# A root multiplied as the exponential's scale: attention with the q norm kept out of q, in a four-layer kernel

## The reference

```python
def rms_norm(x, g):
    return x * lax.rsqrt(jnp.mean(x * x, axis=-1, keepdims=True) + 1e-6) * g

def even_layer(x, ...):
    h = rms_norm(x, norm_g); proj = h @ w_in            # aq ak av ag bq bk bv bg
    aq = apply_rope(rms_norm(aq, a_qn)); ak = apply_rope(rms_norm(ak, a_kn))
    ya = sliding_window_sink_attention(aq, ak, av, sinks) * silu(ag)   # 8 q heads, 2 k heads
    bq = rms_norm(bq, b_qn); bk = rms_norm(bk, b_kn)                   # 8 heads, no rope
    yb = chunked_relbias_attention(bq, bk, bv, b_rel) * silu(bg)
    return x + concat(ya, yb) @ w_out

def odd_layer(x, ...):
    h = rms_norm(x, norm_g); q, k, v, gate = split(h @ w_in)
    q, k = rms_norm(q, qn), rms_norm(k, kn)             # 8 heads x 2 x 64
    s1, s2 = rope(q1) @ rope(k1).T / 8, rope(q2) @ rope(k2).T / 8      # masked by chunks of 64
    o = (softmax(s1) - lam * softmax(s2)) @ v
    y = rms_norm(o, subln_g) * (1 - lambda_init) * silu(gate)
    return x + y @ w_out
```

## Time and profile before

| | |
|---|---|
| median of 3 runs | 1959.96 us (1957.76 to 1960.65) |
| profiled execution, first to last instruction | 1956.6 us |
| so outside that span, against the median | 3.4 us |
| PE busy | 1926.3 us, 98% |
| DVE, ACT, POOL busy | 53%, 51%, 49% |
| first layer, second layer (about) | to 285 us, to 580 us |

### The profile page before, as it was taken

One profiled execution on the slowest core, in us unless ns is written; L12 is line 12 of the kernel. 1 busy time (PEld: TensorE's weight loads), 2 busy tenths in 40 slices (PEclk: granted clock), 3 DMA queues, 4 the chain that ended last, 5 costly groups with the idle time before them and its releaser, 6 DMA issues.

```text
span 1956.6 us, 26922 instructions
## 1 busy us (share of the span) xinstructions
PE 1926.3 (98%) x10034; PEld 1595.6 (82%) x10034; DVE 1028.6 (53%) x1879; ACT 1001.6 (51%) x1770; POOL 952.7 (49%) x1238
## 2 busy tenths in 40 slices
PE   9999999999999999999999999999999999999998
PEld 7877787887788888888788888888889888888887
DVE  4366545666644776576656644402646584444214
ACT  5477546666744555666346444412656364444323
POOL 5542256554554444443554555555543455555553
PEclk9999999999999999999999999999999999999999
DMA  5321122322222222222222232333222223222332
GB/s 201 102 66 53 45 87 87 94 79 81 77 82 95 66 76 76 83 69 76 87 91 91 93 105 97 94 89 100 79 65 63 76 77 107 97 97 97 91 96 73
DMA packets 55379, 169.32 MB, mean 87 GB/s; under 512 B 7120, under 2 KB 14032, under 8 KB 55120
## 3 DMA queue, kind: packets, MB, share of 16 engines
q1 hardware_dynamic: 54960, 167.50, 27.1%
q10 hardware_dynamic: 288, 0.10, 0.0%
HBM read 158.66 MB, written 2.10 MB: 82 GB/s over the span
## 4 chain that ended last, share of the span: by engine, by line
PE 91%; DVE 5%; ACT 2%; POOL 1%; issue 1%; DMA 0%; SPq 0%; ACTq 0%; DVEq 0%
PE ps L1976 23%; PE ps L1979 23%; PE ps L1977 23%; PE ps L2032 3%; PE ps L1988 3%; PE ps L2047 3%; PE ps L1991 2%; PE ps L1989 2%; PE ps L2040 2%; PE ps L2016 1%; PE ps L2026 1%; PE ps L2130 1%; POOL wl L2724 1%; PE ps L2001 1%; PE ps L2004 1%
## 5 line engine op out<-in xcount | busy, mean ns | idle before, releaser
L2724 POOL TENSOR_TENSOR wl<-st,wh 128x256 fp32r<-128x256 f32 (+1 forms) x1180 | 883.6, 780 | 945.8 <-ACT wh L2154 945.1
L1976 PE MATMUL ps<-xh,wh 128*128 128x512 f32 x1432 | 583.5, 407 | 2.5 <-DVE tmp L2412 1.9
L1979 PE MATMUL ps<-xh,wl 128*128 128x512 f32 x1432 | 559.3, 391 | 0.0
L1977 PE MATMUL ps<-xl,wh 128*128 128x512 f32 x1432 | 558.5, 390 | 0.0
L2154 ACT ACTIVATE wh<-st 128x1024 fp32r<-128x1024 f32 (+2 forms) x311 | 314.1, 1011 | 439.3 <-PE ps L1979 390.8
L1976 PEld LDWEIGHTS ps<-xh,wh 128*128 128x128 f32 x1432 | 269.2, 188 | 63.1 <-issue 9.2
L1979 PEld LDWEIGHTS ps<-xh,wl 128*128 128x128 f32 x1432 | 268.8, 188 | 57.6
L1977 PEld LDWEIGHTS ps<-xl,wh 128*128 128x128 f32 x1432 | 269.5, 188 | 54.6 <-issue 5.3
L2683 DVE SCALAR_TENSOR_TENSOR tmp<-ps,vec,tmp 128x510 f32<-128x510 f32 (+1 forms) x176 | 131.2, 749 | 206.5 <-ACT tmp L2333 203.5
L2641 DVE SCALAR_TENSOR_TENSOR res<-res,ps 128x512 f32<-128x512 f32 (+1 forms) x37 | 22.7, 614 | 216.5 <-PE ps L1979 208.2
L1976 PE MATMUL ps<-fa_h,wh 128*128 128x512 f32 x308 | 119.8, 389 | 0.0
(11 more groups left out here) (296 smaller groups left out, 3367.5 us busy)
## 6 DMA issues: line engine op xcount, KB each, us to landing
st<-in_f_up SPq DMA_DIRECT2D x88, 512.0 KB, 3.2
st<-in_o_fm SPq DMA_DIRECT2D x32, 512.0 KB, 3.5
st<-in_s_xbc SPq DMA_DIRECT2D x32, 512.0 KB, 3.5
st<-in_f_dn SPq DMA_DIRECT2D x32, 512.0 KB, 3.5
st<-in_e_fm SPq DMA_DIRECT2D x21, 512.0 KB, 3.5
st<-in_s_z SPq DMA_DIRECT2D x16, 512.0 KB, 3.5
st<-in_s_out SPq DMA_DIRECT2D x16, 512.0 KB, 3.6
tmp<-tmp SPq DMA_DIRECT2D x100, 64.0 KB, 2.0
```

Source lines behind the costliest of these rows:

```text
L1976: e.matmul(u.bank.ap, hi, x.h[:, kk, :], start=first, stop=False)
L1977: e.matmul(u.bank.ap, hi, x.l[:, kk, :], start=False, stop=False)
L1979: e.matmul(u.bank.ap, lo, x.h[:, kk, :], start=False, stop=last).then_inc(S["mm"], 1)
L2724: e.tensor_tensor(P.mem["wl"][w.m % NWR][:, part], P.mem["stage"][w.m % NSTAGE][:, part], P.mem["wh"][w.m % NWR][:, part].bitcast(F32), AL ...
```

## The change

For 12 q units (4 of the first layer's A heads and the 8 of the second layer) the root is no longer multiplied into q. ACT copies the unit with the gain as scale (`q_gain`), and the bank is free when that and the squares are done. The squares are summed per token with the tokens on the partitions: `q_sum`, four matmuls whose stationary side is a 128x128 block of the squares and whose moving side is 2 columns of the matrix of ones. The root of 128x8 numbers (`ln`, `rs`, with 64e-6 for 1e-6, which gives the root with the factor 1/8) stays in a new ring of three small tiles, and is a number per query there. The exponential takes it as its scale, per partition; its bias is minus the greatest score times the root (`mx`, `mx_r`). So the scores of these heads keep their sign, and the mask is minus the large number. The 4 q units of the B heads keep the old way, with the factor -1/8 in the gain.

In the second layer the first three units are k, v, q, where they were q, v, k. Five small kinds of instruction are merged into two (`neg`, `lam`), with the same work.

```diff
+    "pe": (..., "blk", "q_sum", "score", ...
+           "sums": 168, "rec": 177, "q_sum": 480, "mx_r": 160, ...
-        self.turns = ring(["turn0", "turn1"])
+        self.turns, self.roots = ring(["turn0", "turn1"]), ring(mem["rq"])
+        if kind in ("ln", "rs") and n == 8:
+            return 220
+    def q_prep_g(self, u, gain, loaded, pool, done):
+        g = yield from self.taken(self.tmp)
+        g.ready = [(yield ("q_gain", g, u, gain, loaded))]
+        s = yield from self.taken(self.tmp)
+        a = yield ("qsq", s, u)
+        u.bank.release(a, g.ready[0])
+        self.start(4, self.q_root_g(s, a, done))
+        g = yield from self.rope_g(g)
+        dst = yield from self.taken(pool)
+        g.release(*(yield from self.split_q_g(g.ap, g.ready, dst)))
+        done("q", dst)
+    def q_root_g(self, s, squared, done):
+        bank = yield from self.taken(self.aux)
+        t = yield ("q_sum", bank, s, [squared, self.shapes])
+        s.release(t)
+        r = yield from self.taken(self.roots)
+        a = yield ("ln", r.ap, bank.ap[:, 0:8], 1.0, self.c(C_E64, 1), t, r.freed, 8)
+        bank.release(a)
+        r.ready = [(yield ("rs", r.ap, r.ap, a, 8))]
+        done("r", r)
...
 (second layer)
-            prep(0, "qvk"[j], u)
+            prep(0, "kvq"[j], u)
-        yield from P.proj_border_g(x, [w[8], w[24], w[16]], first)
+        yield from P.proj_border_g(x, [w[16], w[24], w[8]], first)
...
-                t = yield ("mn", mn.ap[:, 2 * i:2 * i + 2], g.s, t, mn.freed, 2 * n)
+                t = yield ("mx", mn.ap[:, 2 * i:2 * i + 2], g.s, t, mn.freed, 2 * n)
+                t = yield ("mx_r", mn.ap[:, 2 * i:2 * i + 2], root.ap[:, 2 * i:2 * i + 2], [t, root.ready])
...
 (PE)
+        elif kind == "q_sum":
+            heads = blocks(P.c(C_BLK), 64)[:, :, 0]
+            for i in range(4):
+                t = e.matmul(bank.ap[:, 2 * i:2 * i + 2], cols(s.ap, i), heads, start=True, stop=True,
+                             skip_group_check=True)
 (ACT)
+        elif kind == "q_gain":
+            e.activation(g.ap, u.bank.ap, ACT.Copy, scale=gain).then_inc(S["q_gain"], 1)
-            e.activation(p, s, ACT.Exp, bias=least, scale=-1.0, accum_out=total).then_inc(S["exp"], 1)
+            e.activation(p, s, ACT.Exp, bias=least, scale=scale, accum_out=total).then_inc(S["exp"], 1)
 (DVE)
+        elif kind == "mx_r":
+            e.scalar_tensor_tensor(most, most, -1.0, root, ALU.mult, ALU.mult).then_inc(S["mx_r"], 1)
```

More of the change, by code:

```diff
@@ L62 @@
 STEPS = {
-    "pe": ("raw", "mm", "mm_half", "mm_tok", "ones", "pivot", "blk", "score", "flip", "pv", "feat", "va_t", "dt_t", "cumsum",
+    "pe": ("raw", "mm", "mm_half", "mm_tok", "ones", "pivot", "blk", "q_sum", "score", "flip", "pv", "feat", "va_t", "dt_t", "cumsum",
            "bc_t", "x_t", "cb", "u_mm", "cum_t", "cum_b", "y_mm"),
-    "act": ("w_hi", "table", "sq", "ln", "rs", "split_hi", "gate", "va_in", "qsq", "exp", "sink", "flip_a",
+    "act": ("w_hi", "table", "sq", "ln", "rs", "split_hi", "gate", "va_in", "qsq", "q_gain", "exp", "sink", "flip_a",
             "sub_sq", "lam_e", "conv0", "z_in", "xsilu", "zsilu", "bt", "u_in", "cc_e", "sg_e", "dt_in", "dt_abs",
@@ L1090, in lambdas @@
             lq, lk = (mem["lqk"][:, 128 * j + o:128 * j + o + 64] for o in (0, 64))
-            t = yield ("lam_m", lq, lk, P.lload)
-            t = yield ("lam_r", lam[:, j:j + 1], lq, t)
+            t = yield ("lam", "times", lq, lk, P.lload)
+            t = yield ("lam", "sum", lam[:, j:j + 1], lq, t)
             tl.append((yield ("lam_e", lam[:, j:j + 1], t)))
-        t = yield ("lam_d", lam, tl)
-        P.odd.append((yield ("lam_o", lam, t)))
+        t = yield ("lam", "less", lam[:, 2:3], lam, tl)
+        P.odd.append((yield ("lam", "offset", lam[:, 3:4], lam[:, 2:3], t)))
         P.odd.append((yield ("sub_g", P.V("subln"), P.pload)))
-        P.odd.append((yield ("neg_g", P.V("od_qn"), P.pload)))
     def prep(fb, j, gain, rope, key, pool):
         u = yield from P.proj_g(x, [w[j]])
-        while None in gates.t[0:4] or len(tgain) < 2:
-            yield lambda: None not in gates.t[0:4] and len(tgain) == 2
+        while None in gates.t[0:4] or not tgain:
+            yield lambda: None not in gates.t[0:4] and tgain
+        if rope and key == "q":
+            P.start(4, P.q_prep_g(u, P.V(gain), P.pload, pool, lambda key, dst: got.setdefault(fb, {}).__setitem__(key, dst)))
+            return
         P.start(4, P.qk_prep_g(u, (P.V(gain), tgain), rope, key, pool,
@@ L1202, in attend @@
             kb = 0 if fb < 4 else fb
-            while "q" not in got.get(fb, ()) or "k" not in got.get(kb, ()):
-                yield lambda: "q" in got.get(fb, ()) and "k" in got.get(kb, ())
-            q, k = got[fb]["q"], got[kb]["k"]
+            need = {"q", "r"} if fb < 4 else {"q"}
+            while not need <= got.get(fb, {}).keys() or "k" not in got.get(kb, ()):
+                yield lambda: need <= got.get(fb, {}).keys() and "k" in got.get(kb, ())
+            q, k, root = got[fb]["q"], got[kb]["k"], got[fb].get("r")
             ob = yield from P.taken(P.ob)
@@ L1245, in attend @@
                 P.start(1, back(fb, i, kb0, g, tiles, ob, done))
-            P.start(3, roots(fb, mn, sm, ends))
+            if fb < 4:
+                root.release(*ends)
+            P.start(3, roots(fb, mn, sm, list(ends)))
     y = Acts(yH, yL, 8)
@@ L1271, in prep @@
     def prep(h, key, u):
-        gain, pool = ("od_qn", qs) if key == "q" else ("od_kn", ks)
-        P.start(4, P.qk_prep_g(u, (P.V(gain), tgain), True, key, pool,
-                               lambda dst: got.setdefault(h, {}).__setitem__(key, dst)))
+        put = lambda key, dst: got.setdefault(h, {}).__setitem__(key, dst)
+        if key == "q":
+            P.start(4, P.q_prep_g(u, P.V("od_qn"), P.pload, qs, put))
+        else:
+            P.start(4, P.qk_prep_g(u, (P.V("od_kn"), P.pload), True, key, ks, lambda dst: put("k", dst)))
     def v_post(h, u):
@@ L1342, in attend @@
         for h in range(8):
-            while len(got.get(h, ())) < 2 or tv[h] is None:
-                yield lambda: len(got.get(h, ())) == 2 and tv[h] is not None
-            q, k = got[h]["q"], got[h]["k"]
+            while len(got.get(h, ())) < 3 or tv[h] is None:
+                yield lambda: len(got.get(h, ())) == 3 and tv[h] is not None
+            q, k, root = got[h]["q"], got[h]["k"], got[h]["r"]
             ob = yield from P.taken(P.ob)
@@ L2827, in build @@
         mem["lam"] = at("lam", o + 256, [128, 4])
-        o += 288
+        mem["rq"] = [at(f"rq{i}", o + 288 + 32 * i, [128, 8]) for i in range(3)]
+        o += 384
         R1 = o
```

95 lines of the change are left out of this document (53 added, 42 removed).

## The result

| | before | after |
|---|---|---|
| median of 4 runs each, on one chip | 1959.57 us | 1979.76 us (1978.99 to 1980.68) |
| span of the profiled execution | 1956.6 us | 1978.1 us |

The account below looks back on a forecast made before the run. The prediction took PE, busy 98% of the span, as the bound: its work plus its waits. Terms -0.7 - 1.6 - 1.3 + 4.7 = +1.1 us gave 1961 us, called no change, range 1955.0 to 1966.5.

Parts of the forecast that it names:

- From the third layer on, PE's order is the same instructions in both kernels: Third layer onward: instructions the same in both kernels, so any effect of the change must happen before 560 us.
- The end of the second layer, +4.7: Second layer's tail: last transposes directly behind the last pv, fewer filler steps, PE idle around them; +4.7 us.
- dry tail: Slower rival, second layer's end: nothing repaid ahead of the last head's chain; 1965 us, 1967 with half clock; chance 0.25.
- the four cases: Whole kernel: forecast near 1961 us (0.45), cheaper sums of squares (0.18), PE waits vanishing (0.12), slower second-layer tail (0.25).
- waits ahead that would shrink: Second layer, before its tail: PE's waits were to shrink, with 1.6 us of bank waits and 1.3 us at its begin gone.
- The clock: Second layer's end: if a 5 us hole halves the clock, the next 4 us cost 2 us more, 1967 us.
- PE's work, -0.7: PE, 12 q units: each removed blk costs 0.86 us, each added q_sum 0.80 us; -0.7 us in all.
- cheap sum: Faster rival, PE's q_sum: weight loads at 0.062 us each, 0.50 us per q_sum; 1955 to 1957.4 us; chance 0.18.
- ACT and DVE off the path: ACT and DVE: -4.0 us and about +1.1 us of work, both half free, so neither sum is on the path.
- Bank waits, -1.6: Second layer: PE's three bank waits for the norm's product lose their cause; -1.6 us.
- Begin of the second layer, -1.3: Second layer's start: with order k, v, q, waits of two flips and one transpose vanish; -1.3 us.

Follow-up runs that it names:

- shift96: The kernel before with only its large tiles moved 96 bytes higher in every partition; 1968.21 us, ratio 1.0049.
- old_dry: The kernel before, computation untouched, with the planner's hold at 800 instead of 900 in the first two layers, giving the change's tail order; 1967.37 us, ratio 1.0039.
- align: The changed kernel with the small tiles' area padded to 544 bytes, so large tiles begin at a multiple of 256 bytes again; 1971.45 us, ratio 1.0061.
- ap_scale: The kernel before with the attention exponentials' scale read from a column of -1.0 instead of the number -1.0; 1960.99 us, ratio 1.0011.
- align_qvk: As align, with the second layer beginning q, v, k as in the kernel before; 1971.18 us, ratio 1.0060.
- qsum_twice: As align, with the sum of squares per token done twice in each of the 12 units; 1978.33 us, ratio 1.0099.
- align_warm: As align, with five unused 512-column matmuls added on PE around the second layer's last transposes; 1968.13 us, ratio 1.0044.

## Why the prediction was wrong, step by step

- **Missing altogether: the addresses.** The sum went from instructions to times and took every unchanged instruction at its old time. "From the third layer on, PE's order is the same instructions in both kernels, so whatever the change does must happen before 560 us" was the false sentence: some 9 of the 20 us came behind it (from +12.3 to +21.5 in the table). The addresses alone cost 9.6 us (shift96), and the sum had them at nothing. The diff shows `o += 384` in plain sight.
- **The end of the second layer, +4.7.** The mechanism was right and the size was not. Of the four holes I had two, 2.9 and 2.4 us (measured 2.93 and 2.23). What failed is the chain ahead of the last pv: from the reduction to the pv I had 6.7 us, and it took 559.73 - 551.08 = 8.65, since the transposes stood behind four steps that waited 1.75 us for a bank. So the tail took 567.05 - 551.08 = 16.0 us, not 13.5: +7.1 instead of +4.7. Half clock behind it adds 1.2. The order alone measures +7.6 (old_dry).
- **The rival "dry tail"** had this mechanism, with both its parts, the half clock included, at 0.25 and at 1965 to 1967. It is the nearest of the four cases, and its price was too low as well: the change without the address loss is 1971.5 (align), so the range would have been missed even then. old_dry, at 1967.4, has that mechanism alone. My forecast bet on waits ahead that would shrink. Apart from the three bank waits none did: the flips wait 4.8 us where they waited 3.7.
- **The clock.** I cited the rule on gaps in the matmul stream (Trainium skill, TensorE: Matmul & The Clock Gate, "HAM oscillation — how this bites in real kernels") and let it weigh 2 us in one rival. The trace now agrees in kind inside the kernel: 0.50 behind the holes, worth 1.2 us here and 3.4 in align. In size it differs, and the measurement decides: the page speaks of longer gaps than the holes of 1.4 to 2.9 us here, and behind some of 1.5 to 2.2 us the clock held.
- **PE's work, -0.7.** Mis-sized by little: 0.90 us for a q_sum, not 0.80, so 12 x (0.90 - 0.87) = +0.4. A load costs 0.112 us, near the 0.10 that I chose. The cheap sum by the floor of 62 ns is refuted by the 0.112.
- **ACT and DVE off the path.** The q copy takes 682 ns, not 589, and the exponentials 0.09 us more each, 96 x 0.09 = 8.6 us, which I had left at their old time. By ap_scale this is worth about 2 us (0.4 to 4).
- **Bank waits, -1.6.** Right as far as it goes: the three waits for the norm's product are gone. But a new bank wait of 1.75 us, for the last exponentials, stands in the tail.
- **Begin of the second layer, -1.3.** Wrong: a flip waits 2.2 us at 332 us. With q, v, k it waits less there and more elsewhere (align_qvk), so nothing is gained or lost.

The parts measured alone add to 9.6 (addresses) + 7.6 (order) + 2.2 (columns, for 128 exponentials; here 96) + 0.4 (q_sum) = 19.8 of 20.2 us. They were measured in different kernels, so the agreement is no proof that nothing else is in it. Taken from the other side it is less close: the aligned change is 11.9 us above the kernel before, and order, columns and q_sum make 10.2 of that. Its four more slow matmuls (17 against old_dry's 13) are worth 0.8 more; about 1 us stays open.

## What to carry to other kernels

When a diff moves a buffer, the instructions behind it are not "unchanged": keep every tile that TensorE streams on the step it had (here 256 bytes), and compare start to start the same matmul in both traces. When a planner sets the order, price the new order by itself, with the old computation, before crediting the new one; the last stretch before a layer's end, where the next layer depends on one chain, wants filler steps kept back for it. And a hole there is paid twice when the clock falls behind it, as in align (3.4 us).

## What the hardware showed that I had not expected

- A 512-column matmul in fp32r whose moving tile lies 32 or 96 bytes off the old address takes 233.3 to 233.4 ns from start to start instead of 226.7; 64 bytes off, 230.8. Nothing waits; the cause inside the chip stays open.
- Back-to-back matmul records with a 128x128 load and two moving columns stand 0.112 us apart in qsum_twice, 16 in a row; only the first pair of a row is closer.
- The granted clock fell behind a hole of 1.75 us in align and of 1.37 us in old_dry, and held behind the same 1.75 us in the changed kernel, align_warm and qsum_twice and 1.53 us in the kernel before. What PE did ahead of them was much alike; what decides is open.
